# Expert layer: 32 of 256 tokens by gathered rows on VectorE, 224 densely with the values as stationary operand

## The chip, the cores and the metric

One core of one Trainium2 chip runs the whole kernel. The metric is the device time of one execution in microseconds; three runs of the kernel before stand below.

## The reference, cut to what matters

The kernel computes one block of a hybrid network (retention, RWKV-7 and an expert layer) for 256 tokens of width 2,048 in float32. The change lies in the expert layer, which picks 128 of 16,384 experts for each token (8 heads, 16 each), takes a dot product of the token with each picked row of `expert_u`, applies gelu and the gate, and sums the picked rows of `expert_v` with these weights.

```python
def block(args):
    xb, eb, gb = args
    ue = jnp.take(expert_u, eb, axis=0)
    act = jax.nn.gelu(jnp.einsum('nhkd,nd->nhk', ue, xb), approximate=False) * gb
    return jnp.einsum('nhk,nhkd->nd', act, jnp.take(expert_v, eb, axis=0))
...
x = x + peer(h2, peer_w_q[layer], peer_keys_1[layer], peer_keys_2[layer], peer_u[layer], peer_v[layer])
return rms_norm(x, final_norm_w)
```

## The kernel before, in words

The kernel gathers nothing. It computes the dot products of all 256 tokens with all 16,384 rows of `peer_u` (stage U), multiplies by a gate matrix that is zero where an expert was not picked, and multiplies the result with all of `peer_v` (stage V). Both tables are streamed once, 128 MB each, in units of 512 KB.

To keep float32 accuracy, each matmul operand is split into a rounded high part and a low part (type fp32r), and three products are added: high by high, high by low, low by high. For the weights ScalarE writes the high part `w_hi` (`hi`), and VectorE or GpSimd (POOL) the low part `w_lo` (`lo`, and the loop at the end of POOL's program). `w_hi` and `w_lo` have two buffers, `raw` has four; a unit is split in two halves of 512 columns. SyncE issues all loads, each when the low part of the unit four before is done.

Stage U: 64 iterations (`u_blocks`, `u_lo`, `um`) of four units, each iteration two blocks of 128 experts. The experts are the stationary operand and the tokens are streamed: `mm2` streams high and low activations together (512 columns) past `w_hi`, then the high ones (256 columns) past `w_lo`. POOL makes the low parts of units 0, 2 and 3, VectorE that of unit 1. VectorE adds the two halves of each result (`usum`), ScalarE applies gelu. During the first 21 iterations VectorE also finds the top 16 (`pick_steps`). From iteration 31 on, a "turn" per iteration builds the gates of 8 tokens: one-hot rows by VectorE (`hot_e2`, `hot_e1`), scaled by ScalarE (`hot_gate`), multiplied on TensorE in plain float32 (`gates_mm`), and multiplied into the stored results `big` (`gate_in`, `late_in`).

Stage V: two halves of 1,024 output channels, each 32 iterations of four units. The activations (tokens) are the stationary operand and `peer_v` rows are streamed: 12 matmuls of 512 columns a unit (`v_piece`), into four PSUM banks a half. Per unit ScalarE rounds the activations and splits the weights' high part, VectorE makes both low parts (`v_lo`). After V the result is added to `x1`, read back from DRAM, and the last norm follows (`add_last`, `square_last`, `finish`). In `last_units` the order is chosen so that the first banks are complete early.

The order of work on every engine is its program's order; engines wait for each other by semaphores alone.

Of the kernel before, what the change touches and what calls it, by code (L numbers as in the profile page):

```python
# [5 lines left out]
P = 128  # L6
TOK = 256
# [34 lines left out]
POOL_SLOTS, DVE_SLOTS = (0, 2, 3), (1,)  # L42
# [15 lines left out]
EXP_AT, PICKED_AT, GATE_AT = 21, 23, 31  # L58

EARLY = 2 * GATE_AT  # L60
GATE_TURNS = TOK // 8
# [29 lines left out]
def hybrid_block_kernel(nc, a):  # L91
# [4 lines left out]
    with ctx:  # L96
# [153 lines left out]
        late_out = [cst[:, SIN:SIN + TOK], extra[:, 768:1024]]  # L250
# [54 lines left out]
        def u_split_sem(it, k, halves):  # L305

            if k in DVE_SLOTS:
                return S["u_dve"], it * (2 * len(DVE_SLOTS)) + (2 * DVE_SLOTS.index(k) + halves)
            return S["u_pool"], it * (2 * len(POOL_SLOTS)) + (2 * POOL_SLOTS.index(k) + halves)
# [6 lines left out]
        def _(sp):  # L316
# [94 lines left out]

            def load_u(it):
                for k in range(4):
                    if isinstance(it, int) and it == 0:
                        sp.wait_ge(S["unit_split"], 2 * (U0 + k) - 6)
                    else:
                        sp.wait_ge(*u_split_sem(it - 1, k, 2))
                    sp.dma_start(raw[:, k, :], a["peer_u_t"][ds(it * 2 + k // 2, 1), k % 2]
                                 .rearrange("a p n -> p (a n)")).then_inc(S[f"raw_in{k}"], 16)
            run_loop(sp, 0, BLOCKS // 2, load_u)  # L420

            for h in range(2):
                def load_v(it):
                    for k in range(4):
                        if h == 0 and isinstance(it, int) and it == 0:
                            sp.wait_ge(*u_split_sem(BLOCKS // 2 - 1, k, 2))
                        else:
                            sp.wait_ge(S["unit_split"], it * 8 + (2 * (U0 + h * BLOCKS + k) - 6))
# [4 lines left out]
                else:  # L433
                    run_loop(sp, 0, 10, load_v)

                    sp.wait_ge(S["half_used"], 2 * (V0 + BLOCKS + 24))
                    for piece in range(12):
                        load_v(10 + piece)
# [7 lines left out]
                    with sp.Fori(22, BLOCKS // 4) as it:  # L446
                        load_v(it)
# [10 lines left out]
        def _(pe):  # L458
# [7 lines left out]
            def mm2(bank, wh, wl, kc, start, stop):  # L466
# [4 lines left out]
                if not stop:  # L471
                    last = pe.matmul(PS[:, bank, 0:TOK], wl, act_hi[:, kc, :], start=False, stop=False)  # L472
                return last
# [335 lines left out]
            def um(it, k):  # L809

                for hh in range(2):
                    pe.wait_ge(*u_split_sem(it, k, hh + 1))
# [3 lines left out]
                    for c in range(4):  # L816
                        kc = (k % 2) * 8 + 4 * hh + c
                        cols = slice((4 * hh + c) * P, (4 * hh + c + 1) * P)
                        last = mm2(4 + k // 2, w_hi[:, k % 2, cols], w_lo[:, k % 2, cols], kc, kc == 0, kc == 15)
# [33 lines left out]
            def v_piece(h, k, hh, tt, start, stop):  # L853
                out = PS[:, 4 * h + 2 * tt + hh, :]
                cols = slice(hh * 512, (hh + 1) * 512)
                ah = act_hi[:, k % 2, tt * P:(tt + 1) * P]
                al = act_lo[:, k % 2, tt * P:(tt + 1) * P]
                pe.matmul(out, ah, w_hi[:, k % 2, cols], start=start, stop=False)  # L858
                pe.matmul(out, ah, w_lo[:, k % 2, cols], start=False, stop=False)  # L859
                return pe.matmul(out, al, w_hi[:, k % 2, cols], start=False, stop=stop)  # L860

            def vm(h, it, k, start=False, stop=False):
                u = it * 8 + 2 * (U0 + h * BLOCKS + k)
                pe.wait_ge(S["act2_split"], it * 4 + (h * BLOCKS + k + 1))
                for hh in range(2):
                    pe.wait_ge(S["unit_split"], u + hh + 1)
                    for tt in range(2):
                        last = v_piece(h, k, hh, tt, start, stop)
                    last.then_inc(S["half_used"], 1)

            def last_units():

                for k, tt, hh in ((2, 0, 0), (2, 0, 1), (2, 1, 0), (3, 0, 0), (3, 0, 1), (3, 1, 0), (2, 1, 1), (3, 1, 1)):
                    if tt == 0:
                        pe.wait_ge(S["act2_split"], 2 * BLOCKS - 4 + k + 1)
                        pe.wait_ge(S["unit_split"], 2 * (U0 + 2 * BLOCKS - 4 + k) + hh + 1)
                    last = v_piece(1, k, hh, tt, False, k == 3)
                    if k == 3:
# [1184 lines left out]
```

## Time and profile before

| | |
|---|---|
| three runs | 2,414.74, 2,414.02 and 2,414.70 us |
| the profiled execution | 2,414.85 us, of which the span is 2,412.7 us |
| PE, PEld busy | 2,382.4 us (99%), 2,036.8 us (84%) |
| VectorE (DVE) busy | 1,500.4 us (62%) |
| ScalarE (ACT) busy | 1,363.9 us (57%) |
| GpSimd (POOL) busy | 534.4 us (22%) |
| DMA | 429 MB, 57.2% of the 16 engines' time |

Busy time of an engine counts its compute instructions. PE is TensorE's matmuls, PEld its weight loads, which run beside matmuls. Matmuls overlap, so their durations are longer than the distance between two of them, and it is the distance that makes the time. In a timeline a row has the start in us, the duration, the engine, the line of the kernel and the operation; square brackets hold how long the engine had been idle before and what ended that.

### The profile page before, as it was taken

The numbers are of one execution on the slowest core, as the hardware profiler recorded it, in microseconds if no ns is written. First come the engines' busy times: TensorE is split into PE (matmuls) and PEld (weight loads), VectorE is DVE, ScalarE is ACT, GpSimd is POOL, SyncE is SP. The second block draws the span as 40 slices with busy tenths as digits, with TensorE's granted clock in tenths as the row PEclk, the third lists the DMA queues.
The fourth block names the chain that finished last, engine by engine and source line by source line (L and its number), as shares of the span: only waits on it lengthen the run. The fifth ranks groups of instructions, "written<-read, shape, count | busy, mean of one in ns | idle before, by whom it ended". The sixth has DMA issues, their size and how long they took to land.

```text
span 2412.7 us, 43151 instructions
## 1 busy us (share of the span) xinstructions
PE 2382.4 (99%) x13978; PEld 2036.8 (84%) x13978; DVE 1500.4 (62%) x2694; ACT 1363.9 (57%) x2511; POOL 534.4 (22%) x414
## 2 busy tenths in 40 slices
PE   9999999999999999999999999999999999999998
PEld 8888788978888888888888888888888888888886
DVE  5568988476565655767445555555566666666666
ACT  5456544355544545777776666666555555555555
POOL 0000201100000004666666565565100000000000
PEclk9999999999999999999999999999999999999999
DMA  7665553056656565656565555555556555566654
GB/s 217 185 194 147 166 172 125 21 153 196 193 191 213 164 185 192 189 183 184 186 186 166 168 162 158 169 160 158 184 194 195 192 191 192 193 198 221 213 192 165
DMA packets 187075, 429.09 MB, mean 178 GB/s; under 512 B 13173, under 2 KB 81271, under 8 KB 186103
## 3 DMA queue, kind: packets, MB, share of 16 engines
q1 hardware_dynamic: 186999, 428.07, 57.2%
q8 instruction: 49, 0.80, 0.1%
q14 instruction: 27, 0.22, 0.0%
HBM read 423.82 MB, written 4.19 MB: 177 GB/s over the span
## 4 chain that ended last, share of the span: by engine, by line
PE 64%; issue 25%; POOL 6%; DVE 3%; ACT 1%; DMA 0%; POOLq 0%; ACTq 0%; SPq 0%
PE PS L470 20%; PE PS L858 10%; PE PS L860 10%; PE PS L859 10%; PE PS L472 9%; POOL w_lo L1323 5%; PE PS L827 2%; PE PS L513 1%; PE PS L515 1%; PE PS L514 1%; POOL big L1295 1%; PE PS L469 1%; DVE w_lo L1335 1%; DVE inv L1562 0%; PE PS L463 0%
## 5 line engine op out<-in xcount | busy, mean ns | idle before, releaser
L901 ACT ACTIVATE w_hi<-raw 128x512 fp32r<-128x512 f32 x1576 | 953.8, 626 | 566.5 <-PE PS L472 283.2
L470 PE MATMUL PS<-act_both,w_hi 128*128 128x512 f32 x3104 | 1097.2, 399 | 7.1 <-DVE w_lo L1335 6.1
L1335 DVE TENSOR_TENSOR w_lo<-raw,w_hi 128x512 fp32r<-128x512 f32 x1192 | 790.6, 689 | 448.4 <-ACT w_hi L901 445.8
L472 PE MATMUL PS<-act_both,w_lo 128*128 128x256 f32 x2910 | 815.6, 280 | 0.0
L470 PEld LDWEIGHTS PS<-act_both,w_hi 128*128 128x128 f32 x3104 | 577.5, 188 | 135.5 <-DVE w_lo L1335 7.9
L1323 POOL TENSOR_TENSOR w_lo<-raw,w_hi 128x512 fp32r<-128x512 f32 x384 | 496.7, 1312 | 765.6 <-ACT w_hi L901 755.8
L472 PEld LDWEIGHTS PS<-act_both,w_lo 128*128 128x128 f32 x2910 | 550.1, 189 | 4.4 <-issue 0.2
L858 PE MATMUL PS<-w_hi,act_both 128*128 128x512 f32 x1024 | 398.5, 389 | 1.7 <-DVE w_lo L1335 1.7
L859 PE MATMUL PS<-w_lo,act_both 128*128 128x512 f32 x1024 | 398.4, 389 | 0.0
L860 PE MATMUL PS<-w_hi,act_both 128*128 128x512 f32 x1024 | 398.4, 389 | 0.0
L1241 ACT ACTIVATE act_both<-big 128x256 fp32r (+1 forms) x256 | 106.9, 417 | 319.0 <-PE PS L860 317.3
L1968 DVE TENSOR_TENSOR act_both<-big,act_both 128x256 fp32r<-128x256 f32 x256 | 108.8, 425 | 258.0 <-ACT act_both L1241 258.0
L513 PE MATMUL PS<-w_hi,act_both 128*128 128x512 f32 x576 | 226.8, 394 | 2.2 <-DVE w_lo L1335 2.1
L858 PEld LDWEIGHTS PS<-w_hi,act_both 128*128 128x128 f32 x1024 | 192.2, 188 | 42.1 <-DVE act_both L1968 2.1
L860 PEld LDWEIGHTS PS<-w_hi,act_both 128*128 128x128 f32 x1024 | 192.2, 188 | 40.0
L859 PEld LDWEIGHTS PS<-w_lo,act_both 128*128 128x128 f32 x1024 | 192.2, 188 | 39.9
L515 PE MATMUL PS<-w_hi,act_both 128*128 128x512 f32 x576 | 224.3, 389 | 0.0
L514 PE MATMUL PS<-w_lo,act_both 128*128 128x512 f32 x576 | 224.2, 389 | 0.0
L513 PEld LDWEIGHTS PS<-w_hi,act_both 128*128 128x128 f32 x576 | 108.1, 188 | 27.6 <-DVE w_lo L1335 4.9
L514 PEld LDWEIGHTS PS<-w_lo,act_both 128*128 128x128 f32 x576 | 108.2, 188 | 22.5 <-issue 0.5
L515 PEld LDWEIGHTS PS<-w_hi,act_both 128*128 128x128 f32 x576 | 108.1, 188 | 22.5
L1195 ACT ACTIVATE cst<-cst,extra 128x128 f32<-128x128 f32 x256 | 81.0, 387 | 0.0
(238 smaller groups left out, 1494.8 us busy)
## 6 DMA issues: line engine op xcount, KB each, us to landing
raw<-in_peer_u_t SPq DMA_DIRECT2D x256, 512.0 KB, 3.5
raw<-in_peer_v SPq DMA_DIRECT2D x256, 512.0 KB, 4.2
raw<-in_w_in SPq DMA_DIRECT2D x180, 512.0 KB, 3.7
raw<-in_w_out SPq DMA_DIRECT2D x32, 512.0 KB, 4.1
raw<-in_peer_w_q SPq DMA_DIRECT2D x32, 512.0 KB, 4.4
raw<-in_w_ret_branch SPq DMA_DIRECT2D x16, 512.0 KB, 4.3
raw<-in_w_rwkv_branch SPq DMA_DIRECT2D x16, 512.0 KB, 4.7
big<-in_x SPq DMA_DIRECT2D x2, 1024.0 KB, 6.1
```

The source lines that it names most:

```text
L470: last = pe.matmul(PS[:, bank, :], wh, act_both[:, kc, :, :].rearrange("p w n -> p (w n)"), start=start, stop=stop)
L472: last = pe.matmul(PS[:, bank, 0:TOK], wl, act_hi[:, kc, :], start=False, stop=False)
L513: pe.matmul(out, ah, w_hi[:, slot % 2, cols], start=first, stop=False)
L514: pe.matmul(out, ah, w_lo[:, slot % 2, cols], start=False, stop=False)
L515: last = pe.matmul(out, al, w_hi[:, slot % 2, cols], start=False, stop=last_k)
L858: pe.matmul(out, ah, w_hi[:, k % 2, cols], start=start, stop=False)
L859: pe.matmul(out, ah, w_lo[:, k % 2, cols], start=False, stop=False)
L860: return pe.matmul(out, al, w_hi[:, k % 2, cols], start=False, stop=stop)
L901: act.activation(w_hi[:, slot % 2, hh * 512:(hh + 1) * 512], raw[:, slot, hh * 512:(hh + 1) * 512], ACT.Copy).then_inc(S["unit_hi"], 1)
L1323: pool.tensor_tensor(w_lo[:, k % 2, cols], raw[:, k, cols], w_hi[:, k % 2, cols].bitcast(f32), ALU.subtract).then_inc(S["u_pool"], 1)
L1335: dve.tensor_tensor(w_lo[:, slot % 2, cols], raw[:, slot, cols], w_hi[:, slot % 2, cols].bitcast(f32), ALU.subtract).then_inc(S[done], 1)
L1968: dve.tensor_tensor(act_lo[:, k % 2, :], g, act_hi[:, k % 2, :].bitcast(f32), ALU.subtract).then_inc(S["act2_split"], 1)
```

## The change

The first 32 tokens are served sparsely, the other 224 (`DT`) as before.

- Sparse part. The picked experts' numbers of the 32 tokens (4,096 pairs) are laid out as 32 tiles of 128. For each tile POOL issues an indirect DMA that gathers 128 rows of 8 KB from `peer_u`, and VectorE multiplies and reduces it with the token rows in two halves (`sparse_step`, `tensor_tensor_reduce`); then the same with `peer_v`, where the two halves are scaled by the gated weight and accumulated (`scalar_tensor_tensor`). The U tiles stand in iterations 16 to 33 and every second gate turn, the V tiles in 32 iterations of V. A tile is gathered two iterations ahead, into three places. The sum is added to `x1` in DRAM by four accumulating DMAs, one after the other.
- Dense part. U streams 448 and 224 columns instead of 512 and 256, and has 28 gate turns instead of 32. V is turned round: a tile of 128 channels of `peer_v` is the stationary operand, the activations are streamed (448 and 224 columns), and the output has channels on partitions, one tile in each of the eight PSUM banks. Between the halves, and after the second, the result is summed, transposed on TensorE and, for the first half, added to `x1` in DRAM by POOL.
- Low parts. In V, POOL makes those of units 1 and 3, VectorE those of units 0 and 2 (before: VectorE all four). In U nothing moves.
- Top 16: the first 128 tokens are ranked by iteration 11, the others by iteration 28 instead of all by 21.
- The loops of VectorE and POOL over U's turns and V are written out.

```diff
-POOL_SLOTS, DVE_SLOTS = (0, 2, 3), (1,)
+U_SPLIT = {"p_split": (0, 2, 3), "d_split": (1,)}
+V_SPLIT = {"p_split": (1, 3), "d_split": (0, 2)}
+UPAIRS = BLOCKS // 2
...
-EXP_AT, PICKED_AT, GATE_AT = 21, 23, 31
+SPARSE = 32
+DT = TOK - SPARSE
+GATE_TURNS = DT // 8
+FIRST_EXP_AT, EXP_AT, PICKED_AT, GATE_AT = 11, 28, 30, UPAIRS - 1 - GATE_TURNS
...
-GATE_TURNS = TOK // 8
+PICK_TILES = TOPK * 8 * SPARSE // P
+DOT_AT = [16 + t for t in range(18)] + [GATE_AT + 2 * t for t in range(PICK_TILES - 18)]
+MAC_AT = [66 + 8 * t // 5 for t in range(17)] + [100 + 5 * t // 4 for t in range(PICK_TILES - 17)]
+USED_AT = DOT_AT + MAC_AT
+LANDS = 3
+IDS_AT, ADD_AT, FINAL_AT = 13, 119, 24
...
+            def mm_dense(bank, wh, wl, both, start, stop):
+
+                hi_part = both[:, 0, :]
+                if stop:
+                    pe.matmul(PS[:, bank, 0:DT], wl, hi_part, start=False, stop=False)
+                last = pe.matmul(PS[:, bank, 0:2 * DT].rearrange("p (w n) -> p w n", w=2), wh, both, start=start, stop=stop)
+                if not stop:
+                    last = pe.matmul(PS[:, bank, 0:DT], wl, hi_part, start=False, stop=False)
                 return last
...
-            def v_piece(h, k, hh, tt, start, stop):
-                out = PS[:, 4 * h + 2 * tt + hh, :]
-                cols = slice(hh * 512, (hh + 1) * 512)
-                ah = act_hi[:, k % 2, tt * P:(tt + 1) * P]
-                al = act_lo[:, k % 2, tt * P:(tt + 1) * P]
-                pe.matmul(out, ah, w_hi[:, k % 2, cols], start=start, stop=False)
-                pe.matmul(out, ah, w_lo[:, k % 2, cols], start=False, stop=False)
-                return pe.matmul(out, al, w_hi[:, k % 2, cols], start=False, stop=stop)
+            def v_tile(k, j, start, stop):
+                cols = slice(j * P, (j + 1) * P)
+                return mm_dense(j, w_hi[:, k % 2, cols], w_lo[:, k % 2, cols], act2[:, k % 2], start, stop)
...
+            def turn_first():
+
+                for c in range(8):
...
+                    if c in (0, 4):
+                        pe.wait_ge(S["out_even"], 3 + c // 4)
+                        pe.wait_ge(S["odd_read"], 3 + c // 4)
+                    turn_rows(c, 4)
...
+            def gather(t):
+
+                if t == 0:
+                    pool.wait_ge(S["ids_in"], 16 * 8)
+                if t >= LANDS:
+                    pool.wait_ge(S["used"], 2 * (t - LANDS) + 2)
+                if t >= PICK_TILES:
+                    pool.wait_ge(S["used"], 2 * PICK_TILES)
+                rows, lands = (a["peer_u"][0], land_u) if t < PICK_TILES else (a["peer_v"][0], land_v)
+                j = t % PICK_TILES
+                pool.indirect_dma_start(lands[t % LANDS], None, rows, bass.IndirectOffsetOnAxis(ap=ids[:, j:j + 1], axis=0)).then_inc(S[f"landed{t % LANDS}"], 16)
...
+            def add_sparse():
+                pool.wait_ge(S["used"], 4 * PICK_TILES)
+                for q in range(4):
+                    pool.dma_start(x1_dram[0:SPARSE, :], sparse_out[32 * q:32 * q + 32, :], accum_op=ALU.add).then_inc(S["rows_added"], 16)
+                    pool.wait_ge(S["rows_added"], 16 * (3 + q))
+
+            for g in range(2 * UPAIRS):
+                for t in range(2 * PICK_TILES):
+                    if USED_AT[t] - 2 == g:
+                        gather(t)
...
+                low_parts("u" if g < UPAIRS else "v", g % UPAIRS, U_SPLIT if g < UPAIRS else V_SPLIT, U0 // 4 + g)
+                if g == 96:
+                    add_rows(g)
+                if g == ADD_AT:
+                    add_sparse()
...
-                    run_loop(sp, 0, 10, load_v)
-
-                    sp.wait_ge(S["half_used"], 2 * (V0 + BLOCKS + 24))
+                    run_loop(sp, 0, FINAL_AT, load_v)
+
+                    sp.wait_ge(S["half_used"], 2 * (V0 + BLOCKS + 28))
+                    sp.wait_ge(S["rows_added"], 16 * 6)
...
+            def sparse_step(g, w):
+
+                if g not in USED_AT:
+                    return
+                t = USED_AT.index(g)
+                j, half = t % PICK_TILES, slice(1024 * w, 1024 * w + 1024)
+                if w == 0:
+                    dve.wait_ge(S[f"landed{t % LANDS}"], 16 * (t // LANDS + 1))
+                if t < PICK_TILES:
+                    row = land_u[t % LANDS][:, half]
+                    dve.tensor_tensor_reduce(row, row, xw[:, half], 1.0, 0.0, ALU.mult, ALU.add, dots[:, w, j:j + 1]).then_inc(S["used"], 1)
+                    return
+                row = land_v[t % LANDS][:, half]
...
+                    dve.scalar_tensor_tensor(sparse_out[:, half], row, dots[:, 1, j:j + 1], sparse_out[:, half], ALU.mult, ALU.add).then_inc(S["used"], 1)
...
                     if par == 0:
-                        for k in DVE_SLOTS:
-                            u_lo(i + GATE_AT, k)
+                        u_lo(i + GATE_AT, 1)
+                    sparse_step(i + GATE_AT, par)
...
-            add_last(0, 0)
+            for c in range(8):
+                dve.wait_ge(S["tile_done"], 6 + c + 1)
+                sum_tile(c)
+                if c == 5:
+                    add_last(0, 0)
+            add_last(1, 0)
             add_last(0, 1)
-            add_last(1, 0)
```

## Rows read from the trace of the kernel before

**Rows 1.** The page, the chain that ended last: shares of the span by engine.

```profile
PE 64%; issue 25%; POOL 6%; DVE 3%; ACT 1%; DMA 0%; POOLq 0%; ACTq 0%; SPq 0%
```

**Rows 2.** Windows: length, busy (instructions) by engine, granted clock, DMA share, GB/s.

```profile
930.00:1190.00 260.00, 259.72 (x1472) 225.16 (x1471) 171.37 (x526) 191.30 (x278) 178.12 (x138) 1.00 0.59 182
...
1710.00:2400.00 690.00, 690.00 (x3045) 571.21 (x3044) 435.79 (x767) 372.07 (x764) 0.00 (x0) 1.00 0.61 195
```

**Rows 3.** Stage U: timeline, the chain, and lines (ns min/median/max, starts; idle until).

```profile
975.86 0.28 PE L472 MATMUL PS<-act_both,w_lo 128*128 128x256 f32 x1
...
978.68 0.28 PE L472 MATMUL PS<-act_both,w_lo 128*128 128x256 f32 x1
...
L827 PE MATMUL PS<-cst,onehot x256: 270/275/275, 1293.3 to 1693.5; 128*128 128x128 f32 x128
...
1287.02 0.89 PE PS L827 x8
...
L470 PE MATMUL PS<-act_both,w_hi x3104: 387/395/796, 19.2 to 1704.6; 128*128 128x512 f32 x194
...
  POOL w_lo L1323: 0.3, 1
```

**Rows 4.** Timeline of stage V, units in the middle of its first half.

```profile
1799.98 0.39 PE L858 MATMUL PS<-w_hi,act_both 128*128 128x512 f32 x1
...
1802.02 0.39 PE L858 MATMUL PS<-w_hi,act_both 128*128 128x512 f32 x1
...
1802.31 0.42 ACT L1241 ACTIVATE act_both<-big 128x256 fp32r x1 [1.25 <-PE PS L860]
...
1802.64 1.14 ACT L901 ACTIVATE w_hi<-raw 128x512 fp32r<-128x512 f32 x2
...
1803.29 1.29 DVE L1335 TENSOR_TENSOR w_lo<-raw,w_hi 128x512 fp32r<-128x512 f32 x2
...
1805.42 0.39 PE L858 MATMUL PS<-w_hi,act_both 128*128 128x512 f32 x1
```

**Rows 5.** POOL's low parts in U: timeline, and the line (ns min/median/max).

```profile
960.11 0.63 ACT L901 ACTIVATE w_hi<-raw 128x512 fp32r<-128x512 f32 x1
...
960.82 2.55 POOL L1323 TENSOR_TENSOR w_lo<-raw,w_hi 128x512 fp32r<-128x512 f32 x2 [0.65 <-ACT w_hi L901]
...
L1323 POOL TENSOR_TENSOR w_lo<-raw,w_hi x384: 1278/1297/1494, 918.0 to 1700.1; 128x512 fp32r<-128x512 f32 x192
```

**Rows 6.** Timeline of the one wait of PE at the start of V.

```profile
1708.59 1.29 DVE L1335 TENSOR_TENSOR w_lo<-raw,w_hi 128x512 fp32r<-128x512 f32 x2
...
1709.42 0.47 PE L858 MATMUL PS<-w_hi,act_both 128*128 128x512 f32 x1 [1.67 <-DVE w_lo L1335]
```

**Rows 7.** Line of a VectorE operation with two inputs of 128x1024.

```profile
L1842 DVE TENSOR_TENSOR big<-big,PS x8: 1210/1220/1222, 1017.4 to 1152.3; 128x1024 f32<-128x1024 f32 x8
```

**Rows 8.** Weight loads of 64 and 128 columns; timeline of plain float32 matmuls (the scores).

```profile
L463 PEld LDWEIGHTS PS<-big x1280: 129/135/135, 301.6 to 477.3; 64*64 64x64 f32 x183
...
L802 PEld LDWEIGHTS PS<-big x64: 186/192/192, 922.5 to 929.6; 128*128 128x128 f32 x64
...
922.55 7.41 PE L802 MATMUL PS<-big 128*128 128x128 f32 x64 [1.32 <-DVE big L1421]
```

**Rows 9.** DMA issues (count, KB, us to landing); a line's time to issue (ns).

```profile
raw<-in_peer_u_t SPq DMA_DIRECT2D x256, 512.0 KB, 3.5
raw<-in_peer_v SPq DMA_DIRECT2D x256, 512.0 KB, 4.2
...
big<-x_scratch SPq DMA_DIRECT2D x8, 256.0 KB, 4.6
...
big<-in_peer_keys SPq DMA_DIRECT2D x2, 64.0 KB, 9.3
...
L340 SPq DMA_DIRECT2D raw<-in_w_out x32: 367/368/1782, 717.4 to 805.5; - x32
```

**Rows 10.** Timeline of a gate turn: ScalarE waits for VectorE's sum.

```profile
1501.66 0.42 ACT L1188 ACTIVATE extra<-extra 128x256 f32<-128x256 f32 x1 [1.36 <-DVE extra L1878]
```

More of the change, by code:

```diff
@@ L303, in rot_table, with split_done @@
             return cst[:, col:col + TOK].unsqueeze(1).unsqueeze(1).broadcast_to([P, 2, 2, TOK])
[L305 to L309, printed above, removed]
+        def split_done(stage, it, k, halves):
+            of = U_SPLIT if stage == "u" else V_SPLIT
+            name = "p_split" if k in of["p_split"] else "d_split"
+            before = 0 if stage == "u" else UPAIRS * 2 * len(U_SPLIT[name])
+            return S[name], it * (2 * len(of[name])) + (before + 2 * of[name].index(k) + halves)
         def unit_slot(ku, j, kq):
@@ L445, in _ @@
                                          a["final_norm_w"][q * 512:(q + 1) * 512].partition_broadcast(P)).then_inc(S["fw_in"], 16)
-                    with sp.Fori(22, BLOCKS // 4) as it:
+                    for it in range(FINAL_AT + 6, BLOCKS // 4):
                         load_v(it)
@@ L862, in vm @@
             def vm(h, it, k, start=False, stop=False):
[L863 removed]
                 pe.wait_ge(S["act2_split"], it * 4 + (h * BLOCKS + k + 1))
                 for hh in range(2):
[L866 to L879 removed]
+                    pe.wait_ge(*split_done("v", it + h * (BLOCKS // 4), k, hh + 1))
@@ new lines, in vm @@
+                    for j in range(4 * hh, 4 * hh + 4):
+                        if start and h == 0:
+                            if j in (4, 5):
+                                pe.wait_ge(S[f"gelu{j - 4}"], 2 * UPAIRS - 1)
+                            if j in (6, 7):
+                                pe.wait_ge(S[f"gated{j - 6}"], GATE_TURNS)
+                        if start and h == 1 and j >= 4:
+                            pe.wait_ge(S["rows_act" if j % 2 else "rows_dve"], (j - 4) // 2 + 1)
+                        last = v_tile(k, j, start, stop)
+                        if stop and j % 4 < 3:
+                            last.then_inc(S["tile_done"], 1)
@@ L1194, in hot_gate @@
                     row = hotA[:, 4 * par + t, :]
-                    last = act.activation(row, row, ACT.Copy, scale=eg[:, 2, ds(i * 8 + (4 * par + t), 1)])
+                    last = act.activation(row, row, ACT.Copy, scale=eg[:, 2, ds(i * 8 + (SPARSE + 4 * par + t), 1)])
                 last.then_inc(S[f"hot{par}"], 1)
@@ L1937, in _ @@
                 at, end = (EARLY + (BLOCKS - EARLY) * m // turns for m in (n, n + 1))
-                last = dve.memset(Z(at, end), 1.0)
+                last = dve.memset(G[:, at:end, :], 1.0)
             link(last)
@@ L1943, in _ @@
             gate_turn(1)
[L1944 removed]
+            for i in range(2, GATE_TURNS + 1):
                 gate_turn(i)
[L1946 removed]
             usum(BLOCKS // 2 - 1, 0)
[L1949 to L1961 removed]
```

250 lines of the change are left out of this document (178 added, 72 removed).

## The prediction

> **What bounds the kernel now.** I read the page first, for the chain of waits, then windows by stage, and last the timelines of a few units in each stage. In the stages that change TensorE is busy without a break and its clock is granted in full (1.00, so 2.4 GHz) [rows 2]; busy alone says little, since ends of matmuls are modelled, but the chain runs through PE and its issue for 89% and through POOL for only 6% [rows 1]. So time is worth what TensorE is spared, as long as the others keep up. The changed stages take 1,482 of 2,413 us: U (dense dot products) from about 930 to 1,705, V (weighted values) from there to 2,403. A unit is 512 KB of `raw`. In U it gives 8 pairs of one 512-column and one 256-column matmul. 8 pairs take 978.68 − 975.86 = 2.82 us, 0.353 a pair; late in U a turn takes (1693.5 − 1293.3)/31 = 12.91 us, and less two groups of gate matmuls (0.9 each) that is 11.1 us for 32 pairs, 0.347 a pair [rows 3]. In V a unit gives 12 matmuls of 512 columns; 24 take 1805.42 − 1799.98 = 5.44 us, 0.2267 each, 2.72 a unit [rows 4]. Nothing is waited for there: `w_lo` is ready in time, and DMA engines are about 60% busy at 182 to 195 GB/s [rows 2].
>
> **The change: what TensorE saves.** One 512-column matmul costs 0.2267, so the 256-column one costs 0.347 − 0.227 = 0.120 to 0.126. Both are the columns at 2.4 GHz (213 and 107 ns) and 13 to 19 ns. With 448 and 224 columns they become 0.200 and, by columns alone, 0.107. Against the last stands the weight load: 188 to 192 ns in the trace for 128 columns and 135 for 64 [rows 8], so about 0.85 ns a column, some 108 ns for 128 beside a fixed part that overlaps. A 224-column matmul (93 ns of columns) is the first here that is shorter than the load beneath it; the shortest spacing in the trace with a 128-column load is 7.41/64 = 0.115 us [rows 8]. I take 0.110, between 0.107 and 0.120 (nothing gained on that half). A pair costs 0.310 where V's matmuls set the scale, and 0.037 less than before in U.
>
> On the load itself the Trainium skill speaks against the change: "TensorE: Matmul & The Clock Gate", section "LDWEIGHTS (loading the stationary operand)", gives the columns over 1.2, 107 ns for 128. The slope of the two load rows agrees [rows 8]. Taken as a hard floor it makes the pair 0.307 rather than 0.310, 12 us in all.
>
> U: 64 iterations of 32 pairs = 2,048 × 0.037 = **−75** (−55 with nothing gained on the narrow half, −82 by columns). Gates for 28 turns instead of 32: 8 groups of 0.9 = **−7**. V, if only TensorE counts: 256 units × 8 pairs × 0.310 = 635 against 256 × 2.72 = 696, −61.
>
> **V does not get that.** Units 1 and 3 of each four have their low part moved from VectorE to POOL. Take T as the start of unit u−1 on PE (1802.02). ScalarE rounds the activations from T + 0.29, since it waits for the end of unit u−2, and starts the first half of `w_hi` at T + 0.62; VectorE starts `w_lo` at T + 1.27 and takes 0.65 for a half [rows 4], so it is ready at T + 1.92. POOL starts 960.82 − 960.11 = 0.71 after `w_hi` does and takes 1.28 for a half (2.55 for two) [rows 5]: ready at T + 2.61. PE then needs 0.18 to start (first half of `w_lo` done at 1708.59 + 0.65 = 1709.24, matmul at 1709.42) [rows 6], and a matmul after such a stop takes about 0.08 longer than one in the stream. T + 2.87 against the 2.48 that a unit of the new size lasts: PE is late by 0.39 in every second unit. Two units take 2.48 + 2.87 = 5.35, 128 × 5.35 = 685: **−11** instead of −61. Bounds: POOL in time, −61; POOL at its longest, 1.494 [rows 5], +16.
>
> **What the 32 tokens cost.** They add 64 tiles of 128 gathered rows (8 KB each, 1 MB a tile), two VectorE instructions of 128x1024 a tile: 128 × 1.22 [rows 7] = 156 us of VectorE, spread over 64 tiles' iterations. In V the steps stand at units 1 and 3, where VectorE has lost its low parts: per iteration 4 × 0.4 + 4 × 0.65 + 2.44 = 6.7 of 10.7 us, hidden. In the first part of U VectorE is busy 171 us in 23 iterations, 7.4 each [rows 2], of which 2.7 are low parts and sums; the other 4.7, the top 16, are spread over 28 iterations rather than 21, so 3.5. With 2.44 that is 8.6 of 10.2, hidden. In the gate turns the step at par 0 is put ahead of the sum that ScalarE waits for. It already waits 1.36 there [rows 10]; 1.22 later, its next `w_hi` and POOL's `w_lo` come some 0.5 after PE's need in 14 turns: **+7** (0 to 20).
>
> The gathers are issued by POOL, ahead of unit 0, in the midst of its three units in a row (2, 3, 0): 6 × 1.28 of a 10-us iteration. When it reaches the gather its slack is about 1.1 us (unit 0's halves would be ready 1.1 before need), in the gate turns 0.9 more. No row has a DMA on POOL. The nearest is SP's: 0.37 to issue one, in the longest case 1.78 [rows 9]. At 0.37 nothing is lost, at 1.78 12 us. I take 1.5, near the long end since 128 rows need an address each: 18 × 0.4 = **+7** (0 to 12; more is a rival). In V every gather lies ahead of unit 0, after which POOL waits anyway: 0.
>
> Traffic: U moves 2.1 MB per iteration, with a gather 3.15 MB in 10.1 us, 311 GB/s. At 195 GB/s the engines are busy 0.61 of the time, at 182 0.59 [rows 2], which puts their limit at 308 to 320. 18 iterations touch it; a load may land 2.6 us later than its 3.5 [rows 9] before `w_hi` is late. **+6** (0 to 20).
>
> **The moved ends.** Transposes and summing between the halves of V: PE stands until VectorE has summed tile 4 (three sums of about 0.6, as long as a low part of that width, after the unit's own work), then 16 transposes of 0.11: **+3**. POOL then adds the rows to DRAM and waits for them, 6 to 7 us, of which 2.8 are idle time: **+4** (0 to 8). Last, after iteration 119 POOL adds the sparse result in four DMAs of 256 KB, each awaited before the next, and SP may not load iteration 120 before the last has landed. The nearest row for 256 KB is 4.6 us; bounds 3.5 (SP's load in U) and 9.3 (the keys, 64 KB in short rows) [rows 9]. 4 × 4.6 = 18.4; they start at T + 3.9 (T: unit 2 starts), then a load (4.2), `w_hi` and the low part (1.4), PE 0.2; PE was due at T + 5.35. 3.9 + 18.4 + 5.8 − 5.35 = 22.8, and some 2 us of half clock after such a pause (at the lower level, 1.2 GHz, the longest 512-column matmul shows 796 ns instead of 395 [rows 3]; how long it lasts is a guess): **+25** (20 to 44).
>
> A price from a page alone: the Trainium skill, "DMA: Bandwidth & Descriptors", section "Anatomy of one DMA — SWDGE (gpsimd) path", fits 2.0 us and the bytes over 436 GB/s, so 2.6 us for 256 KB. With it the last term would be an estimated 17 instead of 25. No run here shows it yet.
>
> End: the last eight sums and transposes lie ahead of the last add: a sum (0.62), two transposes and two handovers, and the queueing on VectorE, **+3**. Start of U and V (index copies that POOL waits for, an added `dots` chain): **+3**. Everything before 930 us: 0.
>
> **Sum.** −75 − 7 − 11 + 7 + 7 + 6 + 3 + 4 + 25 + 3 + 3 = −35. The profiled execution took 2,414.85 (span 2,412.7 and 2.15 around it), 0.15 above the median shown; 2,414.85 − 35 = **2,380 us**.
>
> **Rivals.** (A) The sum, 2,345 to 2,405: chance 0.55. (B) POOL is in time in V, because ScalarE or PE's queue runs further ahead than one unit's timeline shows, and V gets its 61: 2,330, down to 2,295 if the waits at the end are short too; for it speaks that PE waited for POOL only 0.3 us in all of U [rows 3]; against it that U has no activation rounding ahead of `w_hi`. 0.20. (C) Slower by POOL's issue of a gather. In U the loss is 18 (x − 1.1) + 14 (x − 2.0); it eats the 35 and the 7 already counted from x = 2.8 us, and at 4 us a gather gives 2,453. For it: 128 rows each need an address of their own; against: SP's 0.37. 0.10. (D) The DMA engines set U's pace while gathers run: at 300 GB/s and 2 us of added latency a gather, 2,400 to 2,430. 0.07. (E) A rounded-fp32 matmul below 256 columns runs at the plain rate. Every one in the trace has 256 or 512, so no row excludes it. Plain fp32 takes two instructions of 0.115 for 128 columns (64 records for the 32 matmuls of the scores) [rows 8], 0.40 for 224: + 0.29 × 4,096 = 3,570. 0.08.
>
> **Numbers.** 0.2% is about 5 us, what this kernel's measurement can tell from no change. Faster: A, B, little of D, 0.77. Same 0.05, slower 0.18 (C, E, most of D). The range 2,310 to 2,440 holds A, most of B, D and the low end of C, 0.82; A's own is 2,345 to 2,405.
>
> **What the profile will show.** The 224-column matmul's spacing, 0.107 to 0.112 (E: 0.4). U's iteration 10.1 us, with a gather 10.5. V: two units in 5.35, PE released by POOL's `w_lo` about 128 times for some 40 us in sum (B: none). POOL's gap at each gather, 1.5 us. One PE gap of 20 to 25 us ahead of iteration 120, eight iterations before the end. What would make the prediction wrong: no POOL wait in V, a gather's issue over 2.8 us, or adds much shorter or longer than 4.6.

## The result, and the profile after

The changed kernel takes 2,490.5 us (median of four runs, 2,490.2 to 2,491.4) against 2,414.4 us for the kernel before beside it: ratio 1.032, 95% interval 1.030 to 1.033. It is 76 us slower, where 35 us faster was forecast.

The page of the kernel after: busy time by engine, the chain that ended last, and POOL's low parts, which are now line 1426 (busy, mean ns of one | idle before); the last row is that of the kernel before.

```profile
PE 2322.5 (93%) x14970; PEld 2067.8 (83%) x14970; DVE 1628.9 (65%) x2605; ACT 1346.0 (54%) x2495; POOL 1038.1 (42%) x744
...
PE 69%; POOL 11%; DVE 8%; ACT 5%; issue 4%; DMA 2%; ACTq 1%; SPq 0%; DVEq 0%
...
L1426 POOL TENSOR_TENSOR w_lo<-raw,w_hi 128x512 fp32r<-128x512 f32 x640 | 925.5, 1471 | 1005.4 <-ACT w_hi L986 995.0
...
L1323 POOL TENSOR_TENSOR w_lo<-raw,w_hi 128x512 fp32r<-128x512 f32 x384 | 496.7, 1312 | 765.6 <-ACT w_hi L901 755.8
```

POOL has risen from 6% of the chain to 11% and VectorE from 3% to 8% [rows 1]. The count of POOL's low parts was meant to grow; their mean was not, and it went from 1,312 to 1,471 ns. The line itself (min/median/max in ns, who waited), and PE's two largest sums of waits for `w_lo` (us in total, times, the longest):

```profile
L1426 POOL TENSOR_TENSOR w_lo<-raw,w_hi x640: 1257/1296/2382, 926.5 to 2469.5; 128x512 fp32r<-128x512 f32 x160
...
  PE PS L524: 107.6, 109
```

```profile
PE PS L524 <- POOL w_lo L1426: 107.6, 109, 8.5
PE PS L524 <- DVE w_lo L1478: 21.3, 3, 20.9
```

The median is the old one, the longest is 2.38 us instead of 1.49 [rows 5]. What such an instance looks like, in the middle of V (L2055 is a sparse step, L2146 the low part of the activations, L1478 VectorE's `w_lo`):

```profile
1834.40 1.28 DVE L2055 SCALAR_TENSOR_TENSOR big<-inv,vec,big 128x1024 f32<-128x1024 f32 x1
...
1834.65 3.55 POOL L1426 TENSOR_TENSOR w_lo<-raw,w_hi 128x512 fp32r<-128x512 f32 x2 [2.70 <-ACT w_hi L986]
...
1836.86 0.47 PE L524 MATMUL PS<-act_both,w_hi 128*128 128x448 f32 x1 [0.83 <-POOL w_lo L1426]
...
1837.10 1.65 DVE L1478 TENSOR_TENSOR w_lo<-raw,w_hi 128x512 fp32r<-128x512 f32 x1
```

VectorE starts 0.25 ahead of POOL and ends at 1835.68. POOL's two low parts take 3.55 instead of 2.55 [rows 5]: the 1.0 that is over is just the rest of VectorE's instruction. TensorE stands still for 0.83. Then it is the other way round. VectorE starts a low part at 1837.10, while POOL's second one runs until 1838.20, and it takes 1.65 instead of 0.65 [rows 4].

This is what the Trainium skill, "SBUF — State Buffer", section "SBUF: two separate sides", states: VectorE has a pair of ports to SBUF of its own and one that it shares with GpSimd, the shared one is a lock held for a whole instruction, and a VectorE instruction with two SBUF inputs needs it against a GpSimd instruction that reads SBUF. The trace agrees, with the 1.0 above. The forecast did not weigh this rule, nor what it would do here.

Distances between the same matmul (or activation) in successive iterations show where the time is. I take 63 iterations of U (from its second) and 63 of V (from its first). Worked out from the timelines, in us:

```
                     U, 63   V, 63    plain U  turn, plain  turn, tile  plain V  V with tile
before               763.9   687.4    11.3     12.9         -           10.9     -
after                756.8   763.1    10.0     11.8         14.2        10.5     11.5 or 12.5
```

TensorE's own rate came as forecast (below). In U 7 us are left of the 82 forecast for it and the gates; V loses 76, and what lies outside these iterations another 7 or 8. V's lengths are counted from activation to activation, which cuts a tile's iteration between its two sparse steps: a length of 12.5 holds the delays of two steps, 11.5 that of one. Counted from TensorE's first matmul of an iteration, 31 of the 32 iterations with a tile take 12.4 or 12.5. So a sparse step of V costs 1.0.

### The profile page after: what moved, and what is told of

It reads as the page before. It is cut to its first block, busy times and chain, and to the rows that moved or that the text cites. A ratio compares the mean times of both kernels' runs of the same rounds, so it can differ in the third digit from the quotient of the medians.

```text
span 2489.6 us, 43408 instructions
## 1 busy us (share of the span) xinstructions
PE 2322.5 (93%) x14970; PEld 2067.8 (83%) x14970; DVE 1628.9 (65%) x2605; ACT 1346.0 (54%) x2495; POOL 1038.1 (42%) x744
## 4 chain that ended last, share of the span: by engine, by line
PE 69%; POOL 11%; DVE 8%; ACT 5%; issue 4%; DMA 2%; ACTq 1%; SPq 0%; DVEq 0%
PE PS L524 24%; PE PS L526 10%; POOL w_lo L1426 9%; PE PS L514 9%; PE PS L567 5%; PE PS L569 5%; PE PS L568 5%; PE PS L516 4%; ACT w_hi L986 3%; PE PS L507 3%; DVE w_lo L1478 3%; PE PS L881 1%; DMA x_scratch<-big 1%; DVE big L2048 1%; POOL big L1398 1%
## 5 line engine op out<-in xcount | busy, mean ns | idle before, releaser
L524 PE MATMUL PS<-act_both,w_hi 128*128 128x448 f32 x4096 | 1344.9, 383 | 131.4 <-POOL w_lo L1426 107.6
L1426 POOL TENSOR_TENSOR w_lo<-raw,w_hi 128x512 fp32r<-128x512 f32 x640 | 925.5, 1471 | 1005.4 <-ACT w_hi L986 995.0
L526 PE MATMUL PS<-act_both,w_lo 128*128 128x224 f32 x3952 | 1051.5, 266 | 0.0
L1478 DVE TENSOR_TENSOR w_lo<-raw,w_hi 128x512 fp32r<-128x512 f32 x936 | 741.0, 814 | 429.9 <-ACT w_hi L986 424.6
L524 PEld LDWEIGHTS PS<-act_both,w_hi 128*128 128x128 f32 x4096 | 771.3, 189 | 244.1 <-POOL w_lo L1426 133.9
L526 PEld LDWEIGHTS PS<-act_both,w_lo 128*128 128x128 f32 x3952 | 759.1, 192 | 0.7
L514 PE MATMUL PS<-act_both,w_hi 128*128 128x512 f32 x1056 | 373.8, 400 | 6.8 <-DVE w_lo L1478 6.0
L2146 DVE TENSOR_TENSOR act_both<-big,act_both 128x224 fp32r<-128x224 f32 x256 | 134.5, 526 | 310.1 <-ACT act_both L1338 310.1
L516 PE MATMUL PS<-act_both,w_lo 128*128 128x256 f32 x990 | 278.8, 282 | 0.0
L514 PEld LDWEIGHTS PS<-act_both,w_hi 128*128 128x128 f32 x1056 | 197.2, 189 | 55.6 <-DVE w_lo L1478 7.9
L567 PE MATMUL PS<-w_hi,act_both 128*128 128x512 f32 x576 | 226.9, 394 | 2.2 <-DVE w_lo L1478 2.1
L568 PE MATMUL PS<-w_lo,act_both 128*128 128x512 f32 x576 | 224.3, 389 | 0.0
L569 PE MATMUL PS<-w_hi,act_both 128*128 128x512 f32 x576 | 224.3, 389 | 0.0
L516 PEld LDWEIGHTS PS<-act_both,w_lo 128*128 128x128 f32 x990 | 187.8, 190 | 1.5 <-issue 0.2
L567 PEld LDWEIGHTS PS<-w_hi,act_both 128*128 128x128 f32 x576 | 108.1, 188 | 27.5 <-DVE w_lo L1478 4.8
L569 PEld LDWEIGHTS PS<-w_hi,act_both 128*128 128x128 f32 x576 | 108.1, 188 | 22.8
L568 PEld LDWEIGHTS PS<-w_lo,act_both 128*128 128x128 f32 x576 | 108.2, 188 | 22.5 <-issue 0.5
```

The source lines that it names most:

```text
L514: last = pe.matmul(PS[:, bank, :], wh, act_both[:, kc, :, :].rearrange("p w n -> p (w n)"), start=start, stop=stop)
L524: last = pe.matmul(PS[:, bank, 0:2 * DT].rearrange("p (w n) -> p w n", w=2), wh, both, start=start, stop=stop)
L526: last = pe.matmul(PS[:, bank, 0:DT], wl, hi_part, start=False, stop=False)
L567: pe.matmul(out, ah, w_hi[:, slot % 2, cols], start=first, stop=False)
L568: pe.matmul(out, ah, w_lo[:, slot % 2, cols], start=False, stop=False)
L569: last = pe.matmul(out, al, w_hi[:, slot % 2, cols], start=False, stop=last_k)
```

## The experiments

All are edits of the changed kernel, and each was timed in turn with the kernel before on the same chip. The table has the medians; U and V are the same 63 iterations.

```
kernel                    us       against before, 95%    U      V
after                     2490.5   1.030 to 1.033         756.8  763.1
tiny_sparse_instr         2375.8   0.982 to 0.986         706.2  701.4
no_gathers                2462.1   1.018 to 1.022         726.9  763.4
v_low_all_vector          2383.7   0.985 to 0.989         759.0  659.6
dots_from_psum            2477.2   1.025 to 1.028         739.4  763.7
dense_floor               2338.2   0.967 to 0.970         691.4  678.9
norm_weight_first         2487.4   1.028 to 1.032         756.9  760.5
gather_after_unit0        2463.8   1.019 to 1.023         725.9  764.0
dots_after_sum            2489.2   1.030 to 1.033         756.1  765.0
one_input                 2399.3   0.993 to 0.996         723.7  703.7
v_all_plus_u_fixes        2342.3   0.969 to 0.973         717.6  657.0
v_all_u_fixes_fw          2332.9   0.965 to 0.969         714.4  651.7
v_all_u_fixes_fw_order    2326.0   0.962 to 0.965         703.2  651.2
```

**1. The sparse instructions made tiny.**

```diff
-                j, half = t % PICK_TILES, slice(1024 * w, 1024 * w + 1024)
+                j, half = t % PICK_TILES, slice(1024 * w, 1024 * w + 8)
```

> Edit of the changed kernel: each of the 128 sparse instructions of VectorE works on 8 columns instead of 1,024; gathers, waits and adds are all kept, and what is left out is nearly all of the sparse tokens' dot products and sums. T1 (VectorE's two-input instructions of 128x1024 and POOL's low parts keep each other out of SBUF, so POOL's w_lo is late): iterations with a tile fall from 11.8-12.4 to about 10.3 in U and from 12.5 to about 10.8 in V, turns with a tile from 14.2 to 12; 18 x 1.8 + 14 x 2.2 + 32 x 1.7 = 118, so about 2,375 us, and POOL's longest low part falls from 2.38 to about 1.5. T2 (the gathers do it, by their traffic or by POOL's time to issue them): 2,470 to 2,490.

Measured −114.6 us: 50.6 in U, 61.7 in V. All of V's iterations with a tile are 10.5, turns with a tile 12.2. T1's number (2,375) and places hold; T2 as the main cause falls. 114.6 / 128 = 0.90 us an instruction.

**2. The gathers left out.**

```diff
-                for t in range(2 * PICK_TILES):
-                    if USED_AT[t] - 2 == g:
-                        gather(t)
...
-                    dve.tensor_tensor_reduce(row, row, xw[:, half], 1.0, 0.0, ALU.mult, ALU.add, dots[:, w, j:j + 1]).then_inc(S["used"], 1)
+                    dve.tensor_tensor_reduce(row, xw[:, 1024 - 1024 * w:2048 - 1024 * w], xw[:, half], 1.0, 0.0, ALU.mult, ALU.add, dots[:, w, j:j + 1]).then_inc(S["used"], 1)
```

> Edit of the changed kernel: the 64 gathers and VectorE's waits for them are left out; VectorE's sparse instructions keep their size and places but read rows that lie in SBUF anyway, so the sparse tokens' results are left out in effect. T1 (the two engines' access to SBUF): only POOL's time to issue goes, some 0.95 in U and 1.22 in V where it is not hidden, 64 x 0.5 = about 30: 2,450 to 2,475 us. T2 (gathers): iterations fall to those without a tile, about 2,375 us.

Measured −28.4, all in U (−29.9). In V 32 MB of gathered rows cost nothing in this kernel: V is the same to 0.3 us. In U the usual iteration with a tile falls from 11.8 to 10.7, a turn with one from 14.2 to 13.2.

**3. Where the gather is issued.**

```diff
             def low_parts(stage, it, of, m):
                 for k in of["p_split"]:
+                    if stage == "u" and k == 2:
+                        gathers_at(it)
```

> Edit of the changed kernel: in U POOL issues a gather after the low parts of unit 0 instead of ahead of them, where VectorE does unit 1 and POOL has a gap; the whole computation is done. Without any gathers the iterations 18 to 33 were 1.1 us shorter and the turns with a tile 1.0. If it is the place of the issue that costs (about 1 us of POOL in the middle of its three units in a row): 32 x 1.0 = -25 to -30, about 2,462 us. If it is the traffic or the descriptors written while VectorE holds the access: under 8 us gained, 2,482 to 2,492.

Measured −26.7, and the usual iteration lengths are those of no_gathers (10.7 and 13.2). So it is the place on POOL, not the traffic. POOL's timeline of the kernel after, around one gather:

```profile
1172.78 7.01 POOL L1426 TENSOR_TENSOR w_lo<-raw,w_hi 128x512 fp32r<-128x512 f32 x4 [1.17 <-ACT w_hi L986]
1179.94 0.95 POOL L1439 DMA_INDIRECT inv<-in_peer_u,vec  x1
1180.91 2.52 POOL L1426 TENSOR_TENSOR w_lo<-raw,w_hi 128x512 fp32r<-128x512 f32 x2
```

Four low parts take 7.01 where 4 x 1.28 are 5.1, and the gather's 0.95 and unit 0's low parts stand behind them with no idle time between. Placed behind unit 0, the gather runs while VectorE makes unit 1's low part and is followed by an idle gap:

```profile
1176.11 0.95 POOL L1446 DMA_INDIRECT inv<-in_peer_u,vec  x1 [0.16 <-issue]
1177.50 3.58 POOL L1433 TENSOR_TENSOR w_lo<-raw,w_hi 128x512 fp32r<-128x512 f32 x2 [0.45 <-ACT w_hi L986]
```

**4. One SBUF input instead of two.** This separates the lock from VectorE's being busy. The edit takes away more than the input: the 128x1024 output becomes one of 128x1. Experiment 5 keeps the output.

```diff
-                    dve.tensor_tensor_reduce(row, row, xw[:, half], 1.0, 0.0, ALU.mult, ALU.add, dots[:, w, j:j + 1]).then_inc(S["used"], 1)
+                    dve.tensor_reduce(dots[:, w, j:j + 1], row, AX.X, ALU.add).then_inc(S["used"], 1)
...
-                    dve.scalar_tensor_tensor(sparse_out[:, half], row, dots[:, 1, j:j + 1], sparse_out[:, half], ALU.mult, ALU.add).then_inc(S["used"], 1)
+                    dve.tensor_reduce(totals[:, w, j:j + 1], row, AX.X, ALU.add).then_inc(S["used"], 1)
```

> Edit of the changed kernel: each sparse instruction of VectorE (but V's first two) is replaced by a tensor_reduce over the same 128x1024 gathered elements, which has a single input; gathers, waits, places and adds stay, and the sparse tokens' results are left out in effect. T1 in its strict form (it is the second SBUF input that shuts POOL out, not VectorE's being busy): V's iterations with a tile fall from 12.5 and 11.5 to 10.5 (-61), U's turns and iterations as with tiny instructions (-50): about 2,378 us, though VectorE's busy time stays near 1,600. Rival (any long VectorE instruction that reads SBUF, or VectorE's load, delays the low parts): above 2,470.

Measured −91.2; the time expected was 21 lower, and U is where that is missing. Lines of V (1,720 to 2,300; busy, mean ns), first of the kernel after, then of this one:

```profile
L1426 POOL TENSOR_TENSOR w_lo<-raw,w_hi 128x512 fp32r<-128x512 f32 x195 | 305.1, 1584 | 232.1 <-ACT w_hi L986 222.7 <-DMA x_scratch<-big 9.4
...
L2055 DVE SCALAR_TENSOR_TENSOR big<-inv,vec,big 128x1024 f32<-128x1024 f32 x38 | 48.6, 1278 | 0.0
```

```profile
L1426 POOL TENSOR_TENSOR w_lo<-raw,w_hi 128x512 fp32r<-128x512 f32 x207 | 263.4, 1293 | 268.9 <-ACT w_hi L986 259.5 <-DMA x_scratch<-big 9.4
...
L2057 DVE TENSOR_REDUCE onehot<-inv 128x1 f32<-128x1024 f32 x40 | 48.5, 1212 | 0.0
```

VectorE's instructions are nearly as long (1.21 against 1.28) and stand in the same places, yet POOL's mean falls from 1.58 to 1.29 and V's iterations are 10.5. In V that is nearly all of it (703.7 against 701.4 with tiny instructions). In U it is most: 33 of the 50.6; turns with a tile stay at 13.3 against 12.2 with tiny ones. That part goes with the length of VectorE's instructions.

The second input is not the only way in which VectorE delays POOL. V's first tile has no earlier sum to add to, so its two steps are a `tensor_scalar` with one SBUF input and an SBUF output. In the kernel after they take 0.75, and each time POOL's pair beside them takes 2.88 or 2.89 instead of 2.55:

```profile
1723.00 0.75 DVE L2052 TENSOR_SCALAR big<-inv,vec 128x1024 f32<-128x1024 f32 x1
1723.26 2.88 POOL L1426 TENSOR_TENSOR w_lo<-raw,w_hi 128x512 fp32r<-128x512 f32 x2 [2.70 <-ACT w_hi L986]
```

That iteration takes 11.2 instead of 10.5, in the kernel after and in this experiment, which leaves the two steps as they are. So this case shows one-input instructions of both kinds: a `tensor_reduce` that leaves POOL alone and a `tensor_scalar` that doesn't.

**5. The token rows read from PSUM.** The same question with the arithmetic kept.

```diff
+                    rows_of_x = x_psum[w] if w == 0 or g < 29 else xw[:, half]
-                    dve.tensor_tensor_reduce(row, row, xw[:, half], 1.0, 0.0, ALU.mult, ALU.add, dots[:, w, j:j + 1]).then_inc(S["used"], 1)
+                    dve.tensor_tensor_reduce(row, row, rows_of_x, 1.0, 0.0, ALU.mult, ALU.add, dots[:, w, j:j + 1]).then_inc(S["used"], 1)
```

> Edit of the changed kernel: in U the second operand of the sparse dot product (the token rows) is copied once to PSUM and read from there: its first half of 1,024 columns in all 32 tiles, its second half in iterations 16 to 28; the rest of stage U and all of V are unchanged, and the whole computation is done. T1 (two inputs in SBUF are what shuts POOL out): same instructions, same load, but POOL's low parts stay at 1.3; iterations 18 to 28 fall from about 12 to about 10.5 (-16), 18 half steps more at 0.9 each (-16): about 2,455 us. T4 (VectorE's load or order): no change, 2,485 to 2,495.

Measured −13.3, in the right direction and less than half of what T1 put on it. In the iterations where both halves read PSUM the lock is gone, though VectorE's instructions still take 1.21 and still write 128x1024 to SBUF: it is the input, not the output. Lines of 1,150 to 1,240, the kernel after and this one:

```profile
L1426 POOL TENSOR_TENSOR w_lo<-raw,w_hi 128x512 fp32r<-128x512 f32 x45 | 70.2, 1581 | 12.8 <-ACT w_hi L986 12.6
```

```profile
L1426 POOL TENSOR_TENSOR w_lo<-raw,w_hi 128x512 fp32r<-128x512 f32 x50 | 63.6, 1296 | 20.8 <-ACT w_hi L986 20.7
```

The iterations fall from 11.8 to 11.1; the rest of the way to 10.0 is the gather (with experiment 3 on top, in experiment 10, most of them take 10.0). The turns with a tile, where only the first half reads PSUM, stay at 14.2: freeing one of two steps gained nothing there, and why was not tested.

**6. V's low parts all on VectorE.**

```diff
-V_SPLIT = {"p_split": (1, 3), "d_split": (0, 2)}
+V_SPLIT = {"p_split": (), "d_split": (0, 1, 2, 3)}
```

> Edit of the changed kernel: in stage V VectorE makes all four low parts and POOL none (p_split empty); the whole computation is done. T1 (mutual blocking): no low part is late any more, plain iterations fall from 10.5 to 9.9-10.1 and those with a tile from 12.5 to about 10.3, POOL no longer holds PE at the adds of rows: V from 763 to about 680, 2,405 us. T4 (VectorE's load itself is the trouble): VectorE gets 64 x 2.6 = 166 us more work, 9.2 of each 10 us in iterations with a tile, its low parts come late behind the sparse instructions, and the time is 2,490 to 2,560.

Measured −106.8 (21 us more than expected), faster than the kernel before by 1.3%. Plain iterations of V are 10.0, those with a tile 10.0 to 11.3. VectorE does more and is seldom late: TensorE's matmuls of U and V wait for its low parts 16 times for 15.1 us in all (same stretch of V):

```profile
L1478 DVE TENSOR_TENSOR w_lo<-raw,w_hi 128x512 fp32r<-128x512 f32 x444 | 286.8, 687 | 44.1 <-ACT w_hi L986 24.7 <-issue 1.0
L2146 DVE TENSOR_TENSOR act_both<-big,act_both 128x224 fp32r<-128x224 f32 x222 | 86.6, 390 | 93.8 <-ACT act_both L1338 93.0
```

In the kernel after the second of these has a mean of 514 ns there, for it too waits for POOL. This edit takes away more than the lock: plain iterations lose 0.5 each as well, the adds of rows (iterations 97 and 98) about 8, and iteration 120 loses 17 (experiment 8).

**7. The dense part alone.** No gathers, no sparse instructions, no adds of the sparse sum.

```diff
-                if g not in USED_AT:
+                if g < 999:
                     return
...
-                if g == ADD_AT:
-                    add_sparse()
```

> Edit of the changed kernel: no gathers, no sparse instructions on VectorE and no adds of the sparse sum; the 224 tokens are served as before, and the 32 sparse tokens get no expert output. By the iterations without a tile (10.0 in U, 11.8 in a turn, 10.5 in V, +9.5 at the adds of rows) U should end near 1,640 and V take 64 x 10.5 + 16 = 690: about 2,355 us (T1, and the forecast's own dense terms: 2,415 - 75 - 7 - 11 + 3 + 4 + 3 + 3 = 2,335). If VectorE's own low parts shut POOL out as much as the sparse instructions do, or the dense part has lost elsewhere, it stays above 2,375.

Measured 2,338.2, 76 us faster than before, where the forecast's dense terms sum to −80 (and I had expected 2,355 by the iterations without a tile). So the dense part did what it was to do, and the 32 tokens cost 152 us instead of the 45 that the forecast gave them: 114.6 for VectorE's instructions (experiment 1), and 37.6 for the rest, of which 22.5 are in V (nearly all in iteration 120, the adds) and 14.8 in U (gathers, and what is left of the tiny steps; the two were not separated).

**8. The four adds.**

```diff
+                        if piece == 4:
+                            sp.wait_ge(S["rows_added"], 16 * 6)
-                        a_, q = piece // 4, piece % 4
+                        a_, q = (2, 0, 1)[piece // 4], piece % 4
```

> Edit of the changed kernel: near the end SyncE first loads the final norm's weights among the loads of two iterations, and waits for the added rows only after that, ahead of reading x1; the whole computation is done. If SyncE's wait is what stops the loads and so TensorE for 20.9 us at iteration 120 (the term of four adds in the forecast): -15 to -20, about 2,472 us. Rival: POOL itself is what is missed, since its low parts of iteration 120 stand behind the same four awaited adds; then the time stays within 5 us of 2,490.

Measured −3.0, the rival's number; iteration 120 falls from 33.9 to 31.0. In the kernel after POOL and PE at iteration 120 are:

```profile
2363.41 0.90 POOL L1452 DMA_DIRECT2D x_scratch<-big  x1
2367.70 0.79 POOL L1452 DMA_DIRECT2D x_scratch<-big  x1 [3.39 <-DMA x_scratch<-big]
2371.89 0.75 POOL L1452 DMA_DIRECT2D x_scratch<-big  x1 [3.41 <-DMA x_scratch<-big]
2376.18 0.76 POOL L1452 DMA_DIRECT2D x_scratch<-big  x1 [3.53 <-DMA x_scratch<-big]
```

```profile
2385.91 0.74 PE L524 MATMUL PS<-act_both,w_hi 128*128 128x448 f32 x1 [20.87 <-DVE w_lo L1478]
```

With SyncE's order changed the loads go on, and now POOL's own low part is awaited, behind its adds:

```profile
2384.23 2.49 POOL L1427 TENSOR_TENSOR w_lo<-raw,w_hi 128x512 fp32r<-128x512 f32 x2 [3.22 <-DMA x_scratch<-big]
```

```profile
2385.54 0.74 PE L525 MATMUL PS<-act_both,w_hi 128*128 128x448 f32 x1 [17.83 <-POOL w_lo L1427]
```

Two queues stood behind the same adds, SyncE's and POOL's. With V's low parts on VectorE (experiment 6) iteration 120 takes 16.8 us instead of 33.9, for POOL has no low parts in V and starts the adds as soon as the last sparse step is done. There SyncE's order counts after all (below).

**9. The order in the gate turns.**

```diff
+                        if par == 1:
+                            sparse_step(i + GATE_AT, 0)
...
-                    sparse_step(i + GATE_AT, par)
+                    else:
+                        sparse_step(i + GATE_AT, 1)
```

> Edit of the changed kernel: in the gate turns the first sparse instruction comes behind VectorE's second sum of the turn and its one-hot rows instead of ahead of that sum; the whole computation is done. If ScalarE's wait for that sum is a part of the 2.4 us that a turn with a tile takes beyond one without (the term of +7 in the forecast): 14 x 0.5 to 1 = -7 to -14, about 2,480 us. T1: it is POOL that is shut out wherever the instructions stand, so within 4 us of 2,490.

Measured −1.3; turns with a tile stay at 14.2. As T1 has it, the order doesn't show in this kernel.

**10 to 12. Put together.** The diffs are those of experiments 6, 3 and 5, then 8 on top, then 9.

> Three edits of the changed kernel together, the whole computation done: V's low parts all on VectorE (2,383.7 alone), the gather behind unit 0's low parts in U (-26.7 alone), the token rows in PSUM for the dots (-13.3 alone). If the three costs are separate they add up: 2,344 us. If the second and third recover the same time twice: 2,352 to 2,360.

> As v_all_plus_u_fixes, and the final norm's weights loaded ahead of SyncE's wait for the added rows. With POOL's low parts gone from V, POOL's awaited adds hold nobody but SyncE, so now the order of SyncE's waits is what counts: iteration 120 (16.8 us with V's low parts on VectorE alone) falls to 10.0 to 11: -6, about 2,338 us. Rival: the loads' own traffic makes the 6.8 us, no change.

> As v_all_u_fixes_fw, and the first sparse instruction of a gate turn behind the turn's second sum. T1: within 4 us of that kernel. If ScalarE's wait for the sum shows once POOL is less late: -7 to -14.

The three gains add up: 2,342.3 where 2,344 was expected. SyncE's order is now worth some 5 (6 expected): iteration 120 falls from 15.0 to 10.0. The medians differ by 9.4, but the runs of the two kernels overlap (2,339 to 2,349 and 2,329 to 2,341), and 3 of it are in U, where nothing was changed. The order in the turns is worth 6.9 by the medians, where T1 expected under 4: turns with a tile fall from 13.2 to 12.4, 14 times. So it had been there, and showed once the larger costs were gone. The last kernel takes 2,326.0 us, 3.6% less than the kernel before (interval 3.5% to 3.8%) with all tokens served. Its page and the longest of PE's waits for `w_lo`:

```profile
PE 2260.6 (98%) x14970; PEld 2051.9 (89%) x14970; DVE 1663.4 (72%) x2863; ACT 1342.7 (58%) x2495; POOL 640.0 (28%) x488
```

```profile
PE PS L525 <- DVE w_lo L1485: 10.8, 17, 2.2
...
PE PS L525 <- POOL w_lo L1434: 6.1, 15, 1.2
```

VectorE is busier than in the kernel after (72% against 65%), and by these rows PE waits 17 us for it and POOL instead of 129. It is below the dense part alone (2,338), which still has V's low parts on POOL: V is 27.7 shorter, U 11.8 longer.

## Why the prediction was wrong

**The step that failed** is in "What the 32 tokens cost": the "156 us of VectorE" from 128 instructions of 1.22, called "hidden". It asked whether VectorE has the time, and it has. It did not ask what VectorE's instruction does to POOL's, which run at the same time. The bound for POOL, "at its longest, 1.494", came from a kernel in which they hardly met: VectorE's long two-input instructions in U read their second operand from PSUM there [rows 7]. The term was 0 and measured 114.6, of which 91.2 go when the instructions have one SBUF input and a small output (experiment 4). Moving the input alone out of SBUF brings POOL's low parts from 1,581 to 1,296 ns (experiment 5), and without POOL's work V's steps cost little (6). Of the 111 us between forecast and result, 107 lie in the terms of the 32 tokens (152 instead of 45).

As an estimate from these rows, each sparse step can hold POOL back for up to its own 1.22 us, 156 us if all meet a low part on the path: 2,380 + 156 = 2,536 at the worst. 0.90 of 1.22 were found. A rival "the 128 steps meet POOL's low parts" was missing.

**What held.** A pair costs 0.314 (0.310 forecast): 13 pairs in 983.87 − 979.79.

```profile
979.79 0.37 PE L524 MATMUL PS<-act_both,w_hi 128*128 128x448 f32 x1
...
983.87 0.37 PE L524 MATMUL PS<-act_both,w_hi 128*128 128x448 f32 x1
```

Rival E is out: with 0.200 for the 448 columns, 0.114 is left for the 224, where E had 0.40. U without the sparse part gained 72.5 of the 82 forecast for pairs and gates; iterations 8, 11, 13 and 28 take 11 to 14 instead of 10.0 (why was not tested). V's plain iteration is 10.5 where two units in 5.35 make 10.7. That POOL would be late there and eat V's gain was right: without POOL it is 10.0 (experiment 6), so B could have come true only with another split. The size was less than forecast, 0.24 in every second unit instead of 0.39, and PE's wait is in no row of waits; it shows in the distance between matmuls, 0.45 and then 0.41 where it is else 0.31:

```profile
2436.84 2.55 POOL L1426 TENSOR_TENSOR w_lo<-raw,w_hi 128x512 fp32r<-128x512 f32 x2 [2.70 <-ACT w_hi L986]
...
2437.74 0.37 PE L524 MATMUL PS<-act_both,w_hi 128*128 128x448 f32 x1
...
2438.19 0.47 PE L524 MATMUL PS<-act_both,w_hi 128*128 128x448 f32 x1
```

V without the sparse part measured −8.5 (63 iterations) where −11 and the +7 of its middle make −4. So U gained less than forecast and V more, and that the dense sum came out at −76 against −80 is in part luck.

**Terms of the wrong size.** The adds of rows: +4 forecast, iteration 97 is 10 us longer (20.5). The path was right, the size wasn't: the forecast had POOL issue and await them in 6 to 7 us, and it took 1.9 to issue and 9.4 to wait; PE then waited 8.5 for the low parts behind them. The adds of the sparse sum: +25 forecast, 23.4 measured (33.9 − 10.5). The number is right in part by luck: 3.9 a piece instead of 4.6, against six us at half clock behind the pause instead of two (granted clock 0.50, so 1.2 GHz):

```profile
2384.89:2391.40 6.51, 5.49 (x19) 5.10 (x20) 1.59 (x3) 2.39 (x7) 2.53 (x2) 0.50 0.95 369
```

But the release named (SyncE's) was only one of two. The gather's issue: x = 1.5 was assumed and is 0.96 to 0.98 in U, so by "18 (x − 1.1)" it should be free; it costs 30 in U with full sparse instructions, and at most 15 with tiny ones. The likely reason is that longer low parts had used up the slack of 1.1 (7.01 instead of 5.1 in the timeline of experiment 3); this is read from the timeline, not tested. Traffic, +6 forecast: with the gather moved on POOL nothing is left to explain (U takes 725.9 with, 726.9 without), so 0 in this kernel. The gate turns' order, +7: 7 once the larger costs were away, 1 before. For rival D, the limit of 308 to 320 GB/s was too low: the window above has 369 at a share of 0.95. Rival C had the right place on POOL and a wrong price.

**Open.** In U 17.5 us remain between one-input and tiny instructions. Most of it is in the turns (14 x 1.1), and the order's 7 in experiment 12 is half of that; the other half was not separated. How a one-input `tensor_scalar` delays POOL was not tested either.

## What to carry to other kernels

Before work is given to an idle VectorE beside a busy GpSimd, count the operands: an instruction with two SBUF inputs can stop GpSimd's low parts for as long as it runs, and they stop it. One input is not always safe; look at GpSimd's durations beside it. A busy share says whether an engine has time, not what it shares with its neighbour; a duration measured where the two never met is no bound. Where both engines prepare TensorE's operands, it can pay to give the whole job to one of them, even the busier one (experiment 6), and to look for what a queue's awaited DMA holds up on each engine that stands behind it.

## What the runs showed of the hardware

- The lock works both ways. POOL's low part of 1.28 us takes up to 2.38 beside a two-input VectorE instruction of 1.21 to 1.28; VectorE's of 0.65 takes 1.65 beside POOL's. Beside a `tensor_reduce` with one SBUF input, or with the second input in PSUM, POOL stays at 1.29 to 1.30 though VectorE works for 1.21. Beside a one-input `tensor_scalar` of 0.75 two of POOL's take 2.88 instead of 2.55.
- An indirect DMA of 128 rows of 8 KB holds POOL 0.95 us where VectorE's instructions are tiny or have one input, 1.13 to 1.16 in the mean in V of the kernel after, and lands after 6.1 us in U and 9.1 in V; 32 of them in V cost TensorE nothing there. The line of their issues, with that of the accumulating ones:

```profile
x_scratch<-big POOLq DMA_DIRECT2D x2, 512.0 KB, 9.2
x_scratch<-big POOLq DMA_DIRECT2D x4, 256.0 KB, 3.9
inv<-in_peer_v,vec POOLq DMA_INDIRECT x22, 9.1
big<-in_peer_u,vec POOLq DMA_INDIRECT x21, 6.1
```

- Two small costs in one chain hide each other. The order of the turns was worth 1.3 us in the changed kernel and 6.9 in the repaired one.
